# Last feed-forward net: the inner features behind the first 256 are computed with the weights stationary and all 256 tokens moving, 128 gate and 128 up columns to a group

## What is computed

```
def swiglu_2(h, w_in, w_out):
    gate, up = jnp.split(h @ w_in, 2, axis=-1)
    return (jax.nn.silu(gate) * up) @ w_out
...
    x = x + g2 * swiglu_2(modulate(rmsnorm_2(x, norm2_g[i]), sh2, sc2), ffn_w_in[i], ffn_w_out[i])
```

## Time and profile before

| | |
|---|---|
| time, median of 3 runs | 911.78 us (911.72 to 911.98) |
| the profiled execution's own time | 911.78 us |
| its span, first to last instruction | 910.0 us |
| PE busy | 899.1 us, 99% of the span, 4258 matmuls |
| DVE, ACT busy | 618.3 us (68%), 462.6 us (51%) |
| mean granted clock of TensorE | 0.997 |

### The profile page before, as it was taken

The page is one execution under the profiler, slowest core; times in us unless marked ns, Lnnn a source line. Parts: engine busy times, 40 slices in busy tenths (PEclk is TensorE's granted clock), DMA queues, the critical chain, the costliest instruction groups (busy, mean ns, idle before and its releaser), DMA issues.

```text
span 910.0 us, 11372 instructions
## 1 busy us (share of the span) xinstructions
PE 899.1 (99%) x4258; PEld 751.7 (83%) x4258; DVE 618.3 (68%) x870; ACT 462.6 (51%) x701; POOL 44.5 (5%) x66
## 2 busy tenths in 40 slices
PE   9999999999999999999999999999999999999996
PEld 7888888888988888888888888887888788888885
DVE  6688887757458867678667777665767755555653
ACT  7565444535578376446544444354444444444440
POOL 0010000013103000000000000001000100000000
PEclk9999999999999999999999999999999999999998
DMA  8787777765545454454687777764755565555541
GB/s 326 255 301 262 271 277 274 285 193 202 175 158 184 162 187 163 161 185 139 222 293 277 282 257 278 284 258 150 249 187 178 185 228 185 187 186 186 181 144 46
DMA packets 55567, 195.74 MB, mean 215 GB/s; under 512 B 6824, under 2 KB 7512, under 8 KB 55512
## 3 DMA queue, kind: packets, MB, share of 16 engines
q1 hardware_dynamic: 54936, 193.57, 60.5%
q10 hardware_dynamic: 576, 1.44, 0.4%
HBM read 193.91 MB, written 1.07 MB: 214 GB/s over the span
## 4 chain that ended last, share of the span: by engine, by line
PE 96%; DVE 1%; issue 1%; DMA 1%; POOL 1%; ACT 0%; POOLq 0%; SPq 0%
PE ps L675 30%; PE ps L677 30%; PE ps L676 30%; PE ps L715 2%; PE ps L625 1%; PE ps L618 1%; DMA t_raw<-in_f_up 1%; PE ps L814 1%; PE ps L830 1%; PE ps L772 0%; PE ps L806 0%; POOL t_sc L1635 0%; PE ps L754 0%; POOL t_sc L1606 0%; PE ps L821 0%
## 5 line engine op out<-in xcount | busy, mean ns | idle before, releaser
L1155 DVE TENSOR_TENSOR t_wl<-t_raw,t_wh 128x1024 fp32r<-128x1024 f32 (+2 forms) x308 | 364.0, 1209 | 148.3 <-ACT t_wh L871 146.4
L871 ACT ACTIVATE t_wh<-t_raw 128x1024 fp32r<-128x1024 f32 (+2 forms) x308 | 310.9, 1045 | 143.3 <-DMA t_raw<-in_f_up 67.7
L675 PE MATMUL ps<-t_wh,t_XH 128*128 128x512 f32 (+2 forms) x656 | 257.5, 393 | 0.3 <-DVE t_XL L1187 0.3
L677 PE MATMUL ps<-t_wh,t_XL 128*128 128x512 f32 (+2 forms) x656 | 253.4, 386 | 0.0
L676 PE MATMUL ps<-t_wl,t_XH 128*128 128x512 f32 (+2 forms) x656 | 253.0, 386 | 0.0
L677 PEld LDWEIGHTS ps<-t_wh,t_XL 128*128 128x128 f32 x656 | 123.1, 188 | 24.9
L675 PEld LDWEIGHTS ps<-t_wh,t_XH 128*128 128x128 f32 x656 | 123.2, 188 | 23.9 <-DVE t_wl L1155 0.7
L676 PEld LDWEIGHTS ps<-t_wl,t_XH 128*128 128x128 f32 x656 | 123.4, 188 | 23.1
L675 PE MATMUL ps<-t_wh,t_YH 128*128 128x512 f32 x288 | 113.5, 394 | 0.0
L677 PE MATMUL ps<-t_wh,t_YL 128*128 128x512 f32 x288 | 112.2, 390 | 0.0
L676 PE MATMUL ps<-t_wl,t_YH 128*128 128x512 f32 x288 | 112.1, 389 | 0.0
(11 more groups left out here) (218 smaller groups left out, 619.6 us busy)
## 6 DMA issues: line engine op xcount, KB each, us to landing
t_raw<-in_f_up SPq DMA_DIRECT2D x132, 512.0 KB, 3.6
t_raw<-in_f_dn SPq DMA_DIRECT2D x66, 512.0 KB, 3.3
t_raw<-in_ada SPq DMA_DIRECT2D x48, 512.0 KB, 4.5
t_raw<-in_mkv SPq DMA_DIRECT2D x8, 512.0 KB, 3.3
t_raw<-in_ga SPq DMA_DIRECT2D x8, 512.0 KB, 3.5
t_raw<-in_gc SPq DMA_DIRECT2D x8, 512.0 KB, 3.4
t_raw<-in_gb SPq DMA_DIRECT2D x8, 512.0 KB, 3.5
t_raw<-in_wo SPq DMA_DIRECT2D x8, 512.0 KB, 3.5
```

The source lines that it names most:

```text
L675: pe.matmul(o, xh, h, start=k == 0, stop=False)
L677: x = pe.matmul(o, xl, h, start=False, stop=k == n - 1)
L871: act.activation(wh[:, m % SPL, 0:w], raw[:, n % RAW, 0:w], ACT.Copy).then_inc(hi_made, 1)
L1155: dve.tensor_tensor(wl[:, n % RAW, 0:w], raw[:, n % RAW, 0:w], wh[:, m % SPL, 0:w].bitcast(F32), ALU.subtract).then_inc(drained, 1)
```

## The change

Group `f3_up0` (the first 256 inner features) is left as it is. The other 2560 are computed in 20 groups `f3_x0` to `f3_x19` of 128 gate columns and the 128 up columns of the same features, in 2 units of 4 chunks. In these groups 128 gate columns (side s = 0) or 128 up columns (s = 1) of a chunk are the stationary operand. `XH` and `XL` become the two halves of one tile `XX`, so that one matmul moves 512 columns, all 256 tokens of the high part and all 256 of the low part, past the high weights; a second moves the 256 tokens of the high part past the low weights. The result has features on partitions: columns 0 to 255 of a bank hold high x high plus low weight x high, columns 256 to 511 high weight x low, and the two halves are still to be added.

The new steps, in the order of one group h: `x_sum(h)`: for each side ACT copies columns 256 to 511 to `sg`, and DVE adds columns 0 to 255 to them; ACT then takes silu of the gates in place. `x_mul(h)`: DVE multiplies gates and ups into `hp`, ACT copies that to `HH`. `x_low(h)`: DVE subtracts to get `HL`. No transposes are needed for these features; `hid_turn` is left for `f3_up0` alone. The banks of group h are free for group h + 2 when DVE's two additions are done. The units stay at 512 KB each, with their columns laid out anew in memory ahead of the kernel.

```diff
+CROSS = ("f3",)
+CROSSES = 20
...
+def per_unit(w):
+
+    return 4 if w == 256 else 2
...
-        out.extend((f"{f}_up{g}", 8, 512) for g in range(11))
+        out.extend((f"{f}_up{g}", 8, 512) for g in range(1 if f in CROSS else 11))
+        out.extend((f"{f}_x{h}", 8, 256) for h in range(CROSSES if f in CROSS else 0))
...
+    def crosses(f):
+
+        for h in range(CROSSES):
+            unit(f"{f}_x{h}", 0, *([("x_mul", f, h - 1)] if h else []))
+            unit(f"{f}_x{h}", 1, *([("x_low", f, h - 1)] if h else [("hid_turn", f, 0)]))
+            S.append(("x_sum", f, h))
...
-            unit(f"{f}_dn0", i, *([("hid_turn", f, 10)] if i == 2 else []), *extra.get(44 + i, ()))
+            own = {2: [("hid_turn", f, 10)]}
+            if f in CROSS:
+                own = {0: [("x_mul", f, CROSSES - 1)], 1: [("x_low", f, CROSSES - 1)]}
+            unit(f"{f}_dn0", i, *own.get(i, ()), *extra.get(44 + i, ()))
...
+            if name[2:4] == "_x":
+                return (up_whole if t else gate_whole).at(name[:2], int(name[4:]))
...
+            def cross(name, i, s):
+
+
+                m, q, n = UNIT_NO[name, i], GROUP_NO[name], K_OF[name]
+                if s == 0:
+                    pe.wait_ge(drained, STREAM_NO[name, i] + 1)
+                if i == 0:
+                    pe.wait_ge(*out_of(GROUPS[q - 2][0], s))
+                o = ps[:, bank_of(name, s), :]
+                for c in range(4):
+                    k, at = 4 * i + c, 256 * c + P * s
+                    h, l = wh[:, m % SPL, at:at + P], wl[:, STREAM_NO[name, i] % RAW, at:at + P]
+                    both_parts = o.rearrange("p (a n) -> p a n", a=2), h, XX[:, :, k, :]
+                    if k < n - 1:
+                        pe.matmul(*both_parts, start=k == 0, stop=False)
+                    x = pe.matmul(o[:, 0:256], l, XH[:, k, :], start=False, stop=False)
+                    if k == n - 1:
+                        x = pe.matmul(*both_parts, start=False, stop=True)
...
+            def x_sum(f, h):
+                if h < 2:
+                    act.wait_ge(*hid_made.at(f, 0, 1))
+                else:
+                    act.wait_ge(*x_made.at(f, h - 2))
+                for s in (0, 1):
+                    name = f"{f}_x{h}"
+                    act.wait_ge(*tile_done(name, s))
+                    act.activation(sg[:, h % 2, s, :], ps[:, bank_of(name, s), 256:512], ACT.Copy).then_inc(*x_side.by(f, h, s))
+                act.wait_ge(*gate_whole.at(f, h))
+                act.activation(sg[:, h % 2, 0, :], sg[:, h % 2, 0, :], ACT.Silu).then_inc(*x_silu.by(f, h))
...
+            def x_sum(f, h):
+
+                name = f"{f}_x{h}"
+                for s, made in ((0, gate_whole), (1, up_whole)):
+                    o = ps[:, bank_of(name, s), 0:256]
+                    dve.wait_ge(*x_side.at(f, h, s))
+                    dve.tensor_tensor(sg[:, h % 2, s, :], o, sg[:, h % 2, s, :], ALU.add).then_inc(*made.by(f, h))
```

More of the change, by code:

```diff
@@ L66, in stream_of @@
     units = []
-    for name, n, _ in GROUPS:
+    for name, n, w in GROUPS:
         if name in ("wo1", "co1"):
@@ L72, in stream_of @@
         else:
-            units.extend((name, i) for i in range((n + 1) // 2))
+            units.extend((name, i) for i in range(-(-n // per_unit(w))))
     out = []
@@ L91 @@
 STREAM_NO = {u: n for n, u in enumerate(STREAM)}
-FINAL_UNIT = {name: UNIT_NO[name, (n + 1) // 2 - 1] for name, n, _ in GROUPS}
+FINAL_UNIT = {name: UNIT_NO[name, -(-n // per_unit(w)) - 1] for name, n, w in GROUPS}
 def width(n):
     name, i = STREAM[n]
-    return 1024 if name == "ada" else W_OF[name] * min(2, K_OF[name] - 2 * i)
+    return 1024 if name == "ada" else W_OF[name] * min(per_unit(W_OF[name]), K_OF[name] - per_unit(W_OF[name]) * i)
 def schedule():
@@ L182, in first @@
                 S.append(("mm", "f1_up0", m, t))
+    def crosses(f):
[3 more added lines that the diff above has]
+            S.append(("x_sum", f, h))
     def ups(f, extra, head):
-        for g in range(11):
+        for g in range(1 if f in CROSS else 11):
             for i in range(4):
@@ L335, in schedule @@
     ups("f3", {}, head("co"))
+    crosses("f3")
     downs("f3", {}, tail)
@@ L391, in build @@
         X = sb("X", [P, 2, D])
-        XH = sb("XH", [P, KC, 256], F32R)
-        XL = sb("XL", [P, KC, 256], F32R)
+        XX = sb("XX", [P, 2, KC, 256], F32R)
+        XH, XL = XX[:, 0], XX[:, 1]
         YH = sb("YH", [P, KC, 256], F32R)
@@ L501, in build @@
         consts = Signal(sem("consts"), ["mhalf", "zero", "ident", "one"])
-        hid_keys = [(f, g) for f in FFNS for g in range(11)]
+        hid_keys = [(f, g) for f in FFNS for g in range(1 if f in CROSS else 11)]
+        cross_keys = [(f, h) for f in CROSS for h in range(CROSSES)]
+        x_side = Signal(sem("x_side"), both(cross_keys))
+        gate_whole, up_whole, x_silu, x_made, x_high, x_done = (
+            Signal(sem(n), cross_keys) for n in ("gate_whole", "up_whole", "x_silu", "x_made", "x_high", "x_done"))
         silu_made, hid_made = Signal(sem("silu"), both(hid_keys)), Signal(sem("hid"), both(hid_keys))
@@ L639, in operands @@
                 return XH, XL, 0
+            def cross(name, i, s):
[14 more added lines that the diff above has]
+                        x = pe.matmul(*both_parts, start=False, stop=True)
+                if s == 1:
+                    x.then_inc(used, 1)
+                elif i == 1:
+                    x.then_inc(tile0, 1)
             def mm(name, i, t):
+                if name[2:4] == "_x":
+                    return cross(name, i, t)
                 m, q = UNIT_NO[name, i], GROUP_NO[name]
@@ L657, in mm @@
                 if name[3:] == "dn0" and t == 0:
-                    pe.wait_ge(*hid_lo.at(name[:2], i))
+                    pe.wait_ge(*(x_done.at(name[:2], 2 * i - 1) if i and name[:2] in CROSS else hid_lo.at(name[:2], i)))
                 if name in ("uq0", "ukv0") and t == 0:
@@ L1283, in hid_turn, with x_mul, x_low @@
                                   ALU.subtract).then_inc(*hid_lo.by(f, g))
+            def x_sum(f, h):
[4 more added lines that the diff above has]
+                    dve.tensor_tensor(sg[:, h % 2, s, :], o, sg[:, h % 2, s, :], ALU.add).then_inc(*made.by(f, h))
+            def x_mul(f, h):
+                if h < 2:
+                    dve.wait_ge(*hid_lo.at(f, 0))
+                dve.wait_ge(*up_whole.at(f, h))
+                dve.wait_ge(*x_silu.at(f, h))
+                dve.tensor_tensor(hp[:, h % 2, 0, :], sg[:, h % 2, 0, :], sg[:, h % 2, 1, :], ALU.mult).then_inc(*x_made.by(f, h))
+            def x_low(f, h):
+                dve.wait_ge(*x_high.at(f, h))
+                dve.tensor_tensor(HL[:, 2 + h, :], hp[:, h % 2, 0, :], HH[:, 2 + h, :].bitcast(F32),
+                                  ALU.subtract).then_inc(*x_done.by(f, h))
             def half(p, j, t):
@@ L1591, in _ @@
                     "mem_turn": mem_turn, "rope1": rope1, "rope2": rope2, "rope3": rope3, "rope5": rope5, "ada_sum": ada_sum, "ada_rows": ada_rows,
-                    "hid": hid, "hid_turn": hid_turn, "half": half, "rms": rms, "gain": gain, "scaled": scaled_, "nturn": nturn, "nsplit": nsplit,
+                    "hid": hid, "hid_turn": hid_turn, "x_sum": x_sum, "x_mul": x_mul, "x_low": x_low, "half": half, "rms": rms, "gain": gain, "scaled": scaled_, "nturn": nturn, "nsplit": nsplit,
                     "xturn2": xturn2, "mk_stat": mk_stat, "lat_stat": lat_stat, "lat_row": lat_row, "lat_turn": lat_turn,
@@ L1802, in add @@
         n, c = k.shape[0], w.shape[-1]
-        if n % 2:
+        p = per_unit(c)
+        if n % p:
             k = np.concatenate([k, np.zeros((1, P, c), k.dtype)], 0)
-        a[name] = k.reshape(-1, 2, P, c).transpose(0, 2, 1, 3).reshape(-1, P, 2 * c)
+        a[name] = k.reshape(-1, p, P, c).transpose(0, 2, 1, 3).reshape(-1, P, p * c)
     def halves(name, w):
@@ L1816, in ffn @@
         g, u = w[:, :FF].reshape(D, 11, 256), w[:, FF:].reshape(D, 11, 256)
-        for j in range(11):
+        for j in range(1 if tag in CROSS else 11):
             add(f"{tag}_up{j}", np.concatenate([g[:, j], u[:, j]], 1))
+        for h in range(CROSSES if tag in CROSS else 0):
+            cut = slice(256 + P * h, 384 + P * h)
+            add(f"{tag}_x{h}", np.concatenate([w[:, :FF][:, cut], w[:, FF:][:, cut]], 1))
         halves(f"{tag}_dn", down)
```

5 lines of the change are left out of this document (4 added, 1 removed).

## The result

The changed kernel takes 920.07 us (median of 4 runs, 919.99 to 920.2) against 911.75 us of the kernel before beside it (911.65 to 911.98): a ratio of 1.0091, 95% interval 1.0079 to 1.0103. It is 8.3 us slower. The prediction had said 909.4 us.

What follows compares the result with a forecast made beforehand. TensorE, busy 99% of the span, was taken to bound the kernel by its own instructions. Matmuls +2.1 us and transposes -4.5 us gave -2.4 us, from 911.78 to 909.4 us; 8-in-10 range 907.9 to 911.8.

Steps and rivals of the forecast that it cites:

- The transposes, 4.5 us: On TensorE in the last net, five blocks of 8 transposes at 0.90 us each go, saving 4.5 us.
- The added matmuls, 2.1 us: On TensorE in the 20 groups, 640 matmuls replace 480 over the same columns; their fixed parts add 2.1 us.
- a line through rows of equal length: TensorE matmul price from rows of 512, 384 and 288 columns: columns at 2.4 GHz plus about 13.3 ns.
- The predicted 120.0 ns for 256 columns: Price of each short matmul in the new groups, 106.7 + 13.3 ns, with no such dense row in the trace.
- held up by their loads: Rival, chance 0.18: stationary loads delay the short matmuls in the groups; 911.5 us halfway, 913.6 us at the upper bound.
- The 0.11 us between two loads: Distance between two load starts behind transposes, taken to show a load fits behind 256 columns with 10 ns to spare.
- What is hidden, forecast as nothing: In the groups, VectorE's 4.12 us and ScalarE's 3.64 us fit in TensorE's 5.55 us, so they add no time.
- a constant 1.1 us against a slack of 6.9: Banks are freed about 1.1 us after a group; TensorE writes them again 6.9 us later, leaving 5.8 us.
- The rival of a wait at the banks: Rival, chance 0.06: TensorE waits at each f3_x start for additions two groups before; 915.4 us at 0.3 us a group.
- The prediction's own sign of being wrong: The forecast is wrong if a matmul of 256 columns in the new groups costs more than 122 ns.
- that of a wait for `t_sg`: Sign in the profile after: TensorE waiting for `t_sg` would show the rival of a wait at the banks.
- The first group's transposes: Transposes of f3_up0, now needed at about 734.8 us, would not wait, since its product is done at 730.28.

Runs made afterwards that it cites:

- e4: The kernel before without 40 of the last net's 44 transposes and their copies and subtractions, second product reading only two chunks: 907.34 us.
- e12: e1 with a chunk's high and low parts side by side, and each unit's eight long matmuls in a row, then its eight short ones: 909.82 us.
- e8: e1 with a chunk's high and low parts side by side, and tokens held stationary in place of weights in the 20 groups: 911.21 us.
- e6: e1 with a chunk's high and low parts side by side, and four long matmuls then four short ones instead of alternating: 910.65 us.
- e5: The changed kernel in its own order, with VectorE's subtraction of x_low made twice: 925.76 us.
- e1: The changed kernel with silu of each group moved behind ScalarE's next split: 911.22 us, ratio to the kernel before 0.9994.
- e7: The changed kernel with silu left in place and ScalarE's copy to HH moved behind its next split: 911.13 us.

## Why the prediction was wrong

**The transposes, 4.5 us:** right, 4.4 measured in e4.

**The added matmuls, 2.1 us:** the mechanism was right, a fixed part for each of 160 more, but the price of a pair was taken off a line through rows of equal length: 346.7 ns. It is 352, so 320 x 5.3 ns = 1.7 us are missing. In rows of sixteen the line comes out at 347.8 (e12). The predicted 120.0 ns for 256 columns was right by itself: 120 ns is the commonest step of the short ones there. The rival "held up by their loads" had the right size but another place: the short ones were cheaper than forecast (117), the long ones dearer, and neither the held operand (e8) nor the place behind a short one (e6) decides. The 0.11 us between two loads was weak ground for it, for the matmul recorded from 749.08 on the earlier trace rows lies between the two. On the load the Trainium skill, "TensorE: Matmul & The Clock Gate", section "LDWEIGHTS (loading the stationary operand)", gives 106.7 ns; e12's short ones follow each other every 120 ns with a load each, so a load does fit there, and nothing here shows it as the limit.

**What is hidden, forecast as nothing:** this is the step that failed. The prediction compared sums of busy time, 4.12 and 3.64 us, with the 5.55 us of a group, and took the path from a group's end to its free banks as a constant 1.1 us against a slack of 6.9. The sums were right, but the path was not. The lists of ScalarE and VectorE wait for each other twice a group in either direction, and once round takes 6.33 us. The delay therefore grows by 6.33 - 5.62 = 0.71 us with each group.

The slack was mis-sized too: it was 3.6 us, not 5.8. In both lists `x_sum` of group 0 stands behind `hid_turn`, whose transposes come only behind the group, so the addition that was to follow side 0 (733.39 and 0.24 us) starts at 736.91. With the 0.56 us from there to TensorE that is a path of 3.8 us in place of 1.1, and group 2 starts at 741.03, 3.6 us later. 3.6 / 0.71 = 5.1: the additions of group 5 are just in time, those of group 6 are late, and they hold group 8, the first that waits (eight groups are ahead of it). In e5 the slack is the same and the delay grows by 6.66 - 5.62 = 1.04 us, 3.6 / 1.04 = 3.5: the additions of group 4 are late and hold group 6, as measured. The expectations of e1 and e5 came near the right counts (8 groups, 5 to 6) with 5.8 us by luck, for they counted from the start of the net and not from the first addition.

From group 8 on TensorE stands at 13 starts (12 groups and `f3_dn0`). From the last matmul to the next start these are 0.80 to 0.93 us in place of 0.235, in all 8.2 us more, and some 0.07 us in the step behind each. (The 5.7 us of the table of waits are less, because a matmul's recorded duration still runs when the next could start.) The rival of a wait at the banks named the place, and got 0.06, because it asked for hand-overs of over 6.9 us. It needed only a round longer than TensorE's group, and a net long enough to use up the slack. The prediction's own sign of being wrong, over 122 ns for 256 columns, did not come (117 to 120); that of a wait for `t_sg` did.

**The account:** -4.4 for the transposes, +2.1 and +1.7 for the matmuls, +8.2 and 13 x 0.07 = 0.9 for the waits make +8.5 us; measured +8.3. The waits are shown by e1 (-8.9 us when they go, 9.1 by this account), so the sum closes within 0.3 us.

**The first group's transposes** did not wait, and the DMA and the clock were as forecast.

## What to carry to other kernels

Where two engines with in-order lists hand work to each other more than once per round, add up the longest way round through both lists, from a step back to the same step one round later, and compare that with the round of the engine that sets the pace; busy shares of 59% and 52% say nothing about it. Such a delay shows only once the buffers' slack is used up, so the engine that sets the pace looks free in the first groups. The distance from one of the ring's own steps to the same step a group later shows it at once (6.33 us here from group 0 on, where TensorE took 5.62). And slack is to be counted from where the first such step really stands, with what is ahead of it in its list. The cure cost no instruction here: move the step that waits for the other engine behind one that is ready (e1, e7). And in this kernel matmuls of equal length were cheapest in long rows (e12).

## What the hardware showed that was not expected

A matmul's price depended on the length of those before it. Steady rows cost their columns at 2.4 GHz and 13.3 ns (226.7, 173.2 and 133.2 ns for 512, 384 and 288 columns, 120 for 256). After a change of length, or after transposes, long ones took 224 to 241 ns, in a few patterns that recur, whatever operands they held or moved, in one piece or two, and with the elementwise engines at full or short work. The steady price was back after five equal ones in e12 and after two or nine in the kernel before. The short ones between were slightly cheaper than in a steady row (117 against 120 ns). Alternating 512 and 256 columns cost 352 ns a pair, rows of four 351, rows of sixteen 348. What in the engine does this stays open; no run looked inside.
